# Decay matrices of a chunked state-space scan kept in PSUM, and the first group of chunks reordered

## What is computed

```python
def ssd_chunked(X, A, B, C):                      # per direction; chunks of 128 tokens
    a_cs = jnp.cumsum(A, axis=2)
    seg = a_cs[:, :, :, None] - a_cs[:, :, None, :]
    l_mat = jnp.exp(jnp.where(mask, seg, -jnp.inf))          # the decay matrix of a chunk and head
    y_diag = jnp.einsum('bclgn,bcsgn,bclsgj,bcsgjp->bclgjp', C, B, l_mat, X)
    states = jnp.einsum('bclgn,bclgj,bclgjp->bcgjpn', B, decay_states, X)
    ...                                                       # scan of the states over the chunks
    y_off = jnp.einsum('bclgn,bcgjpn,bclgj->bclgjp', C, prev, jnp.exp(a_cs))
    return y_diag + y_off
```

## Time and profile before

| | before |
|---|---|
| runs shown | 3097.46, 3086.70, 3087.19 us |
| median | 3087.19 us |
| profiled execution: its own time | 3090.69 us |
| its span (first to last instruction) | 3088.8 us |
| PE busy over the span | 3002.6 us (97%) |
| DVE, POOL, ACT busy | 1873.4, 1493.4, 1130.1 us |
| mean granted TensorE clock | 0.992 |

### The profile page before, as it was taken

How to read it: one execution, slowest core, us unless ns; L and a number is a source line. 1 busy time by engine, 2 the same in 40 slices (tenths; PEclk the granted TensorE clock), 3 DMA queues, 4 the chain that set the end, 5 groups by cost and what they waited for, 6 DMA issues and landing times.

```text
span 3088.8 us, 48812 instructions
## 1 busy us (share of the span) xinstructions
PE 3002.6 (97%) x18926; PEld 2709.7 (88%) x18926; DVE 1873.4 (61%) x2742; ACT 1130.1 (37%) x1977; POOL 1493.4 (48%) x924
## 2 busy tenths in 40 slices
PE   8999999999999999999999999899999999999997
PEld 8999999999999999999999988576667788887776
DVE  6677777745433334345788842588888944445665
ACT  4466566632333332102111122233333533334552
POOL 4100000053766775444444444477675477776773
PEclk9999999999999999999999999999999999999998
DMA  3010000021222223221233423332323233335442
GB/s 126 25 37 28 27 26 16 26 94 44 78 80 84 80 74 125 104 84 48 95 121 93 133 82 118 109 120 90 118 90 114 69 107 101 100 102 176 148 128 80
DMA packets 173449, 270.44 MB, mean 88 GB/s; under 512 B 13350, under 2 KB 83238, under 8 KB 173222
## 3 DMA queue, kind: packets, MB, share of 16 engines
q1 hardware_dynamic: 133472, 219.74, 21.3%
q10 hardware_dynamic: 39749, 47.60, 4.6%
HBM read 200.53 MB, written 66.75 MB: 87 GB/s over the span
## 4 chain that ended last, share of the span: by engine, by line
PE 79%; DVE 7%; POOL 6%; issue 4%; DMA 1%; ACT 1%; SPq 1%; DVEq 0%; POOLq 0%; ACTq 0%
PE PS L1258 71%; PE PS L1514 4%; PE PS L1499 2%; DMA Wraw<-in_w 1%; POOL Wlo L1157 1%; POOL SQ L1202 1%; POOL Wlo L1104 1%; POOL RMS L1167 1%; POOL SQ L1197 1%; PE PS L1847 1%; DVE MX L2978 0%; DVE GD L3533 0%; POOL STB L1189 0%; PE PS L1995 0%; SPq L870 0%
## 5 line engine op out<-in xcount | busy, mean ns | idle before, releaser
L1258 PE MATMUL PS<-Uhi,Whi 128*128 128x352 f32 (+2 forms) x1992 | 506.7, 333 | 17.2 <-DVE Ulo L2770 13.8
L1258 PE MATMUL PS<-Uhi,Wlo 128*128 128x352 f32 (+2 forms) x1992 | 501.4, 330 | 0.0
L1258 PE MATMUL PS<-Ulo,Whi 128*128 128x352 f32 (+2 forms) x1992 | 501.3, 330 | 0.0
L1063 POOL TENSOR_TENSOR Whi<-Wraw,const 128x1024 fp32r<-128x1024 f32 x84 | 207.8, 2474 | 546.9 <-PE PS L1258 520.0
L1258 PEld LDWEIGHTS PS<-Uhi,Whi 128*128 128x128 f32 x1992 | 337.9, 189 | 40.7 <-issue 17.4
L1258 PEld LDWEIGHTS PS<-Ulo,Whi 128*128 128x128 f32 x1992 | 340.7, 189 | 20.0
L1258 PEld LDWEIGHTS PS<-Uhi,Wlo 128*128 128x128 f32 x1992 | 340.7, 189 | 19.4
L1104 POOL TENSOR_TENSOR Wlo<-Wraw,Whi 128x512 fp32r<-128x512 f32 x200 | 270.4, 1356 | 92.7 <-ACT Whi L2402 92.6
L1145 POOL TENSOR_TENSOR Olo<-H,Ohi 128x1056 fp32r<-128x1056 f32 x5 | 12.1, 2444 | 521.8 <-ACT Ohi L2305 521.8
L1258 PE MATMUL PS<-T,Whi 128*128 128x264 f32 (+1 forms) x1456 | 254.7, 303 | 1.1 <-DVE SQ L3171 0.6
L1066 POOL TENSOR_TENSOR Wlo<-Wraw,Whi 128x1024 fp32r<-128x1024 f32 x84 | 234.2, 2788 | 6.6
(11 more groups left out here) (407 smaller groups left out, 6912.6 us busy)
## 6 DMA issues: line engine op xcount, KB each, us to landing
Wraw<-in_w SPq DMA_DIRECT2D x232, 256.0 KB, 2.9
Wraw<-in_w SPq DMA_DIRECT2D x91, 512.0 KB, 3.6
xt<-XTT ACTq DMA_DIRECT2D x20, 640.0 KB, 5.6
Wraw<-in_w SPq DMA_DIRECT2D x88, 128.0 KB, 2.7
Ulo<-opd SPq DMA_DIRECT2D x17, 512.0 KB, 5.3
H<-in_x ACTq DMA_DIRECT2D x16, 528.0 KB, 8.1
zt<-ZB ACTq DMA_DIRECT2D x32, 256.0 KB, 2.0
X<-xt SPq DMA_DIRECT2D x8, 1024.0 KB
```

The source lines that it names most:

```text
L1063: pool.tensor_tensor(Whi[s][:], Wraw[s][:], ones.unsqueeze(1).broadcast_to([P, BLK, P]), ALU.mult)\
L1258: ins = pe.matmul(out, lhsT, rhs, start=start, stop=stop, skip_group_check=True)
```

## The change

- ACT no longer copies the exponents to SBUF: `take_decays` and the semaphore `l_ready` go (64 ACT instructions). `choose` writes the lower triangle into PSUM bank `2h` itself, `exponentials` works in place in that bank, and `weigh_bc` reads it from there and writes `M`. `decays(n)` and the last user of bank 2 now wait for `m_ready` of the step before instead of `cp_done`; `weigh_bc` takes over the wait on `y_full` that protects `M`.
- In group 0 the first forward read goes to bank 6 and the backward reads to bank 7 (`read_bank`), so they don't wait for bank 5. PE issues the read of step 0 after job 1 and `decays(1)` after job 4; DVE does `weigh_bc(0)`, `read(0, 0)` and `choose(1)` between the jobs, and `diagonal(0)` ahead of `read(0, 1)`. During group 0 DVE weighs the jobs of group 1 one place earlier, and `diagonal(1)` moves from step 1 to the end of step 2.
- `LHS[1]` and `BTOK[1]` change places in SBUF. Both `LHS` tiles are now set ahead of the first `cleared`; SP loads group 1 when `z_full` says that the last gate matmul is done.

```diff
+    def read_bank(n, d):
+        return 5 if n >= CPS else 7 if d else 5 if n else 6
@@ SP
-                    sp.wait_ge(cleared, 2)
+                    sp.wait_ge(z_full, GROUPS * WIN)
@@ PE decays
-                    pe.wait_ge(cp_done, 2 * (n - 1) + h + 1)
+                    pe.wait_ge(m_ready, 2 * (n - 1) + h + 1)
@@ PE, jobs of group 0
             chunk_state(0, q)
+            if q == 1:
+                read_state(0, 0, 0, STF[:, 0, :])
+            if q == 4:
+                decays(1)
@@ PE, steps
-            if k < CPS - 1:
+            if k < CPS - 1 and i:
                 pe.wait_ge(o_taken, READS * i + 2 * k + 1)
-                read_state(i, k, behind(i, k))
+                read_state(i, k, 1, behind(i, k))
+            elif k < CPS - 1:
+                if k:
+                    pe.wait_ge(o_taken, 2 * k)
+                read_state(i, k, 1, behind(i, k))
@@ ACT
-                act.activation(half(n, h), PS[:, 2 * h, :], ACT.Copy).then_inc(l_ready, 1)
...
-                act.activation(half(n, h), half(n, h), ACT.Exp).then_inc(e_ready, 1)
+                act.activation(PS[:, 2 * h, :], PS[:, 2 * h, :], ACT.Exp).then_inc(e_ready, 1)
@@ DVE, constants
-            if k == 0:
-                step(vec.tensor_tensor(LHS[k][:]...
+            step(vec.tensor_tensor(LHS[k][:]...
...
-        vec.tensor_tensor(LHS[1][:]...).then_inc(cleared, 1)
@@ DVE choose
-                vec.wait_ge(l_ready, 2 * n + h + 1)
-                vec.copy_predicated(M[n % 2][:, h * HALF:(h + 1) * HALF, :],
+                vec.wait_ge(f_full, 2 * n + h + 1)
+                vec.copy_predicated(PS[:, 2 * h, :].rearrange("p (h l) -> p h l", h=HALF),
@@ DVE weigh_bc
-                vec.tensor_tensor(m, m, G[i % 2][:, k, :]..., ALU.mult)
+                if n >= 2:
+                    vec.wait_ge(y_full, n - 1)
+                vec.tensor_tensor(m, PS[:, 2 * h, :]..., G[i % 2][:, k, :]..., ALU.mult)
@@ DVE, jobs of group 0
-        for q in range(JOBS):
+        take_state(0, 0)
+        weigh(0, 2)
+        weigh_bc(0)
+        for q in range(1, JOBS):
             take_state(0, q)
             if q + 2 < JOBS:
                 weigh(0, q + 2)
-        read(0, 0)
-        weigh_bc(0)
+            if q == 2:
+                read(0, 0)
+            if q == 4:
+                choose(1)
+        diagonal(0)
         read(0, 1)
-        diagonal(0)
@@ DVE, steps
+            if k and i == 0:
+                weigh(1, 2 * k - 1)
             if 1 <= n <= SCAN:
                 take_outputs(n - 1)
...
-                weigh(i + 1, 2 * k - 1)
+                weigh(i + 1, 2 * k - (i > 0))
...
-            if k == 1 and i < last:
+            if k == 1 and 0 < i < last:
                 diagonal(i + 1)
...
+            if n == 2:
+                diagonal(1)
```

More of the change, by code:

```diff
@@ L495, in encoder @@
             YThi = sb("YThi", [P, CPS, SEQ], F32R, s2)
-            BTOK = [sb(f"BTOK{k}", [P, CPS + 1, P], F32, s2) for k in range(2)]
+            BTOK0 = sb("BTOK0", [P, CPS + 1, P], F32, s2)
             BCH0, CCH0 = (sb(n, [P, SEQ], F32, s2) for n in ("BCH0", "CCH0"))
             YTlo = sb("YTlo", [P, CPS, SEQ], F32R, s2)
-            LHS0 = sb("LHS0", [P, 2, SEQ], F32R, s2)
+            LHS = [sb(f"LHS{k}", [P, 2, SEQ], F32R, s2) for k in range(2)]
             RH = [sb(f"RH{k}", [P, 2, HPG, CK], F32R, s2) for k in range(2)]
@@ L1977, in chunk_state, with read_state @@
             mm(PS[:, bank, :], BTOK[i % 2][:, c_, :], XW[(JOBS * i + q) % 2][:]).then_inc(s_full, 1)
-        def read_state(i, k, state):
-            mm(PS[:, 5, :], CCH[i % 2][:, k * CK:(k + 1) * CK], state).then_inc(o_full, 1)
+        def read_state(i, k, d, state):
+            mm(PS[:, read_bank(CPS * i + k, d), :], CCH[i % 2][:, k * CK:(k + 1) * CK], state).then_inc(o_full, 1)
         def chunk_outputs(n):
@@ L2043, in _ @@
             r = i - 1
-            if n + 1 < SCAN:
+            if n == 0:
+                pass
+            elif n + 1 < SCAN:
                 decays(n + 1)
@@ L2047, in _ @@
                 pe.wait_ge(row_ready, c.want(row_ready))
-                pe.wait_ge(cp_done, 2 * SCAN)
+                pe.wait_ge(m_ready, 2 * SCAN)
                 spread_half(0, FACTOR_BANKS[0]).then_inc(ssd_rms, 1)
@@ L2086, in _ @@
                 if i < last:
-                    pe.wait_ge(o_taken, READS * i + 2)
+                    pe.wait_ge(o_taken, READS * i + 2 if i else 1)
                     products_bc(i + 1)
@@ L2101, in _ @@
                 if i < last:
-                    pe.wait_ge(o_taken, READS * i + min(2 * k + 2, READS))
+                    pe.wait_ge(o_taken, READS * i + min(2 * k + 2, READS) if i else 2 * k + 1)
                     chunk_state(i + 1, 2 * k)
@@ L2649, in _ @@
         take_bc(0)
-        take_decays(0)
         exponentials(0)
@@ L3475, in _ @@
             two = ident[:, 2 * HPG:2 * HPG + 2]
-            if k == 0:
-                step(vec.tensor_tensor(LHS[k][:].rearrange("p d t -> p (d t)"), two[:, 0:1].broadcast_to([P, 2 * SEQ]),
-                                       two[:, 1:2].broadcast_to([P, 2 * SEQ]), ALU.add))
+            step(vec.tensor_tensor(LHS[k][:].rearrange("p d t -> p (d t)"), two[:, 0:1].broadcast_to([P, 2 * SEQ]),
+                                   two[:, 1:2].broadcast_to([P, 2 * SEQ]), ALU.add))
         vec.sem_inc(cleared, 1)
         vec.wait_ge(z_full, GROUPS * WIN)
-        vec.tensor_tensor(LHS[1][:].rearrange("p d t -> p (d t)"), two[:, 0:1].broadcast_to([P, 2 * SEQ]),
-                          two[:, 1:2].broadcast_to([P, 2 * SEQ]), ALU.add).then_inc(cleared, 1)
         last = GROUPS * NSEQ - 1
@@ L3633, in _ @@
             if k and i < last:
-                weigh(i + 1, 2 * k - 1)
-            if n + 1 < SCAN:
+                weigh(i + 1, 2 * k - (i > 0))
+            if 0 < n and n + 1 < SCAN:
                 choose(n + 1)
```

24 lines of the change are left out of this document (9 added, 15 removed).

## The result

| | before | after |
|---|---|---|
| median of six runs each | 3088.76 us | 3070.07 us |
| lowest to highest | 3086.42 to 3097.46 | 3068.39 to 3071.14 |
| profiled execution: its own time, its span | 3090.69, 3088.8 us | 3068.39, 3066.4 us |
| ratio after to before | | 0.9934, 95% interval 0.9921 to 0.9948 |

The changed kernel is faster by 0.66%, 18.7 us between the medians. The forecast was 3070.4 us, and the likeliest case was the one that came.

What follows compares the result with a forecast made beforehand. PE, busy 97% of the span, was taken as the bound, so only its waits could shrink. Steady groups 10.5, group 0 6 and last group 0.3 make 16.8 us; 3087.2 less that is 3070.4 us, range 3061 to 3084.

Steps and rivals of the forecast that it cites:

- the likeliest case: Whole kernel: the forecast itself, 3070.4 us, its own range 3066 to 3075; chance 0.50.
- Product out of PSUM: DVE's 64 products: 0.68 us each instead of a median of 1.67, bounds 0.66 and 1.78.
- Steady groups: Six group ends after group 0: earlier state add and gate shorten PE's waits, 1.75 us each, 10.5 us in all.
- Predicated copy into PSUM: DVE's copy with its target moved to PSUM: 0 change, bounds -0.05 and +0.65 us an instruction.
- The new wait: PE's decay matmuls wait for the previous step's product: costs nothing at 0.68 us, about 0.1 us a step at old durations.
- Group 0: First group of the scan, up to PE's first turn: 6 us gained, between 2 and 8.
- Step 3: Group 0's fourth output step: 1.8 us gained, 1.6 if the clock stands at 2.4 GHz and 0.2 of contention.
- At nothing: Remaining parts priced at 0: setting LHS[1] earlier, covered by DVE's idle time, group 1's loads, and the last m_ready wait.
- B: DVE: stretching persists with a PSUM source, or the predicated copy pays its upper bound, 9 us; 3084 us, chance 0.13.
- C: Steady part as forecast, but group 0 gives only 1 to 3 us; 3074.4 us, chance 0.20.
- D: POOL's sums shrink to 1.28 us and nearly all PE waits go, 3 us a group; 3061 us, chance 0.08.
- E: Slower: bank held until a product of 1.78 us or longer ends, deciding above 2.5 us a pair; 3105 us, chance 0.07.

Runs made afterwards that it cites:

- kernels with one bank: Changed kernel with group 0's backward reads in bank 5 again: 3067.28 us; the same plus the next group's diagonal moved to the end of step 1: 3067.13 us.
- the halves: Kernel before with only the product read from PSUM: 3078.23 us; kernel after with only that undone, so order, banks and places alone: 3089.59 us.
- the one with the late diagonal: Changed kernel with the next group's diagonal moved, in groups 1 to 6, to the end of step 1: 3066.23 us once, 3063.09 us with more runs.

## Why the prediction held, and where it did not

*Product out of PSUM: right.* 0.68 us taken, 0.682 measured, no stretching. The kernels with the second input in SBUF and with the product made twice show that this one number carries the steady gain.

*Steady groups: right in mechanism, too small in size.* 1.75 us a group forecast, 2.13 measured, 12.9 instead of 10.5 us. The order of the waits came as written: no state add, gate below its old wait, XW still 0.6. The gate's wait was put at 0.4 to 0.6 and is 0.3. The waits by the profile explain 1.2 us of the 2.13 (2.1 to 0.9 a group); another 0.8 lies in time that counts as busy, since PE is busy for 49.49 us of a period before and 48.69 after with the same matmuls. The forecast allowed 0.2 us for what a modelled end hides. That is the term to widen.

*Predicated copy into PSUM: right number, wrong reason.* I took 0; it became 41 ns cheaper, 0.04 within the bound of 0.05. But "no row has DVE write PSUM" was an oversight: the trace of before has such lines in the feed-forward part, of nearly the same size, and they would have put the new copy at about 0.68 to 0.71 us and made the upper bound of +0.65 needless. One of them, kernel before:

```profile
L3160 DVE TENSOR_TENSOR PS<-GATE,PS x40: 680/698/714, 795.0 to 2821.7; 128x528 f32<-128x528 f32 x20, 128x512 f32<-128x512 f32 x20
```

*The new wait: nothing in the steady groups, as said.* It was looked at only at a group's end. In group 0 it would have cost 1.47 us had the order stayed; the forecast never asked, because it took the order as given.

*Group 0: 6 us forecast, 7.2 measured, with errors that cancel in part.* First taking: 4.1 forecast, 4.8 measured. Step 1: 3.0 and 2.95. Step 2: -1.3 and -1.0. Step 3: 1.8 and 0.3. Last stretch to the turn: -0.6 and +0.2. The step that failed is the clock of step 3: "1.6 us of that go if the clock stands at 2.4 GHz there". It did not; the matmuls took 3.68 us as they had taken 3.49. The kernels with one bank, where it stood at 2.4 GHz during those matmuls, have a ring of 7.29 us; they pay for it in step 1. The 1 us taken off for not being able to place the clock was about that size. That the terms ahead of this deduction add up to 7.0 against 7.2 is thus no sign that each was right.

*Who earns group 0: not asked, and it should have been.* The forecast's terms read as if the order earned them. Alone it earns 2.6 us. The short product is a condition of the rest.

*At nothing: LHS was not at nothing.* The forecast had put 1.2 us at the start of group 0 into its first term, rightly in kind and too large in size (0.7 us at the turn, 0.85 at the first taking). It had put 0 for the loads; nothing in the traces speaks against that, and it was not tested by itself.

*The last group:* 0.3 forecast, 0.8 measured.

*The rivals.* B (the price of the PSUM target, or stretching from the writing side) falls by the lines. C expected a slow clock in group 0, at another place; it came at the same step as before, and group 0 still gave 7.2 and not 1 to 3 us. D said that POOL's sums shrink and nearly all of PE's waits go: they shrank, and by the doubled product this moved nothing. E needed a pair above 2.5 us; it takes 1.28. Its threshold was wrong besides: at 2.7 us a pair, with the product made twice, PE does not wait for the product in a steady group.

The median came out 0.3 us from the forecast because two deviations cancel: the gain between the two groups of six runs was 18.7 us for a sum of 16.8, 1.9 more, and the median of the kernel before was itself 1.6 us above the one that the forecast started from. By the trace the three stages that were forecast gained 20.9 us (7.2, 12.9 and 0.8). The mechanism is borne out; that closeness is luck.

## What to carry to other kernels

A DVE instruction that stretches beside POOL is found by its minimum and median: where they are far apart at one shape, look at whether both its inputs are in SBUF, and take one of them from PSUM or move the instruction to where POOL rests. Both did it here, and the second costs nothing but an order. And look for the price of an unusual operand in the whole trace, not only in the stage that is changed.

A change with an order and a data path in it is best priced as a pair: the halves gave 2.6 and -0.4 us in the first group, the whole 7.2.

## What the runs showed of the hardware

- The stretching does not scale with the instruction: four DVE operations of 8 numbers a partition took 4.68 us beside POOL, one of them as long as 2260 ns, where they take 227 each undisturbed. Each of the last three ends with a POOL instruction: the longest runs from 1997.83 to 2000.09, and a POOL instruction of 2.33 us beside it ends at 2000.07. For their length, small ones lose most. The line in the kernel with the diagonal of group 1 in step 3:

```profile
L3538 DVE SCALAR_TENSOR_TENSOR KAP<-DT,DIAG,SKIPR x32: 225/227/2260, 1968.7 to 2276.4; 128x8 f32<-128x8 f32 x32
```

- PSUM as source and target at once is the cheapest form of two lines: the predicated copy 690 ns against 731 into SBUF, the exponential 582 against 632 from SBUF to SBUF. A table of the Trainium skill (VectorE: DVE Perf Modes, section on the TRN2 errata) has a PSUM source cost 62 cycles more than an SBUF one (120 against 58 of overhead); the rows do not bear it out for this product, 682 ns from PSUM against 679 at the least from SBUF.
- Where the granted clock falls in a stretch in which PE has gaps depends on small things ahead of it. The kernel after and the one with the late diagonal run the same program up to the first turn; step 3 was at the 1.2 GHz level in both, but the latter, in both of its executions (on two chips), was partly there from step 1 on (0.85 and 0.81 over 20 us, and 1.3 us more for group 0). What decides it stays open; no run here was made for it.
